# Second mixer's pairs: the inverse's transposed block from a swapped product, four groups per pair, values copied last, ScalarE fading the state

## The reference, cut to what matters

```python
a_mat = where(strict, (k*beta) @ k.T * decay, 0)
t_mat = solve_triangular(a_mat + eye, eye)         # the inverse
u = t_mat @ (v * beta);   w = t_mat @ (k*beta * exp(gc))
def step(state, inp):                              # over the chunks, in order
    v_new = u - w @ state
    o = q_dec @ state + qk @ v_new
    state = state * exp(g_last) + k_dec.T @ v_new  # fade, then add
```

## Time and profile before

| what | value |
|---|---|
| median of 3 runs | 1034.4 us (1032.77 to 1034.87) |
| the profiled execution's own time | 1036.71 us |
| its span in the trace | 1034.9 us |
| mean granted TensorE clock | 0.994 of full |
| busy: PE / DVE / ACT / POOL | 97% / 62% / 42% / 19% |
| pairs of half 0 in the span | about 797.6 to 862 us |
| pairs of half 1 in the span | about 923.0 to 988 us |

### The profile page before, as it was taken

One profiled execution on the slowest core, in us unless ns is written; L12 is line 12 of the kernel. 1 busy time (PEld: TensorE's weight loads), 2 busy tenths in 40 slices (PEclk: granted clock), 3 DMA queues, 4 the chain that ended last, 5 costly groups with the idle time before them and its releaser, 6 DMA issues. The chain is left out here.

```text
span 1034.9 us, 14694 instructions
## 1 busy us (share of the span) xinstructions
PE 1007.5 (97%) x5678; PEld 815.5 (79%) x5678; DVE 645.1 (62%) x1075; ACT 432.9 (42%) x875; POOL 194.1 (19%) x166
## 2 busy tenths in 40 slices
PE   8999999999999999999999999999999998999997
PEld 5888888888776677788878888888888777888886
DVE  4154566622237778767836866686497777967726
ACT  4222323423258863342533343455433466235432
POOL 0011000000001253100100001200203565114692
PEclk9999999999999999999999999999999999989999
DMA  9267634232413252242414346544333212133402
GB/s 320 81 225 259 228 114 151 82 122 82 150 45 113 73 200 101 62 142 82 152 61 160 122 143 231 185 136 144 120 143 123 83 62 85 59 123 105 162 2 81
DMA packets 60820, 132.25 MB, mean 128 GB/s; under 512 B 6096, under 2 KB 6480, under 8 KB 60624
## 3 DMA queue, kind: packets, MB, share of 16 engines
q1 hardware_dynamic: 58304, 118.67, 34.0%
q0 software_dynamic: 2304, 12.58, 3.3%
q10 hardware_dynamic: 144, 0.07, 0.0%
HBM read 117.09 MB, written 14.22 MB: 127 GB/s over the span
## 5 line engine op out<-in xcount | busy, mean ns | idle before, releaser
L289 DVE TENSOR_TENSOR w_lo<-raw,w_hi 128x2048 fp32r<-128x2048 f32 x56 | 132.0, 2357 | 212.1 <-ACT w_hi L285 196.1
L285 ACT ACTIVATE w_hi<-raw 128x2048 fp32r<-128x2048 f32 x51 | 97.4, 1912 | 195.2 <-PE projections_ps L125 156.9
L123 PE MATMUL projections_ps<-projections_x_hi,w_hi 128*128 128x512 f32 x208 | 81.1, 390 | 0.4 <-ACTq L649 0.4
L124 PE MATMUL projections_ps<-projections_x_lo,w_hi 128*128 128x512 f32 x208 | 80.9, 389 | 0.0
L125 PE MATMUL projections_ps<-projections_x_hi,w_lo 128*128 128x512 f32 x208 | 80.9, 389 | 0.0
L123 PE MATMUL projections_ps<-w_hi,projections_x_hi 128*128 128x512 f32 x192 | 74.9, 390 | 0.0
L125 PE MATMUL projections_ps<-w_hi,projections_x_lo 128*128 128x512 f32 x192 | 74.7, 389 | 0.0
L124 PE MATMUL projections_ps<-w_lo,projections_x_hi 128*128 128x512 f32 x192 | 74.7, 389 | 0.0
L246 DVE SCALAR_TENSOR_TENSOR resid<-resid,mixer_cw 128x512 f32<-128x512 f32 x96 | 64.9, 745 | 0.0
L123 PE MATMUL projections_ps<-w_hi,output_m_hi 128*128 128x512 f32 x128 | 51.2, 400 | 2.2 <-DVE resid L1572 1.2
L750 POOL TENSOR_TENSOR tok<-tok,attention_recip 128x512 f32<-128x512 f32 x8 | 8.3, 1043 | 229.8 <-DVE attention_recip L839 229.8
(11 more groups left out here) (371 smaller groups left out, 2416.5 us busy)
## 6 DMA issues: line engine op xcount, KB each, us to landing
raw<-in_w_in SPq DMA_DIRECT2D x26, 1024.0 KB, 5.0
raw<-in_gdn_w_in SPq DMA_DIRECT2D x24, 1024.0 KB, 5.0
tok<-in_ada_w POOLq DMA_DIRECT2D x16, 768.0 KB, 6.4
raw<-in_w_out SPq DMA_DIRECT2D x8, 1024.0 KB, 5.0
qkv_kept<-mixer_ring SPq DMA_DIRECT2D x8, 1024.0 KB, 4.2
mixer_st<-qkv_kept SPq DMA_DIRECT2D x32, 256.0 KB, 2.9
raw<-in_gdn_w_out SPq DMA_DIRECT2D x7, 1024.0 KB, 5.5
resid<-in_att_bias SPq DMA_DIRECT2D x16, 256.0 KB, 2.7
```

The source lines that it names most:

```text
L123: nc.tensor.matmul(out, w_hi, x_hi, start=first, stop=False, skip_group_check=True)
L124: nc.tensor.matmul(out, w_hi, x_lo, start=False, stop=False, skip_group_check=True)
L285: self.nc.scalar.activation(self.hi[s][:], self.raw[s][:], ACT.Copy).then_inc(self.hi_ready, 1)
L289: engine.tensor_tensor(self.lo[s][:], self.raw[s][:], self.hi[s][:], ALU.subtract)\
```

## The change

The transposes "T" and the two scaled copies that follow them are gone. In their place, at level 0, TensorE makes beside each Z0 block a third 32x32 product with its two operands swapped; it gives the off-diagonal block of `T` in the other orientation, and VectorE scales it into `T` with one operation for the whole pair. The diagonal 32x32 blocks of `T` come from `Tc` by two ScalarE activations (`diagonal`), and the block of zeros is set once for each half by GpSimd. Level 1's Z goes to the banks of `psA`, no longer to those of the values. The parts of the next pair move to other slots, and the values are copied at slots 13 and 14. ScalarE multiplies the state by its decay in place (`s_faded`, two activations, chunks 1 and 2), and VectorE only adds, in one operation for both heads.

```diff
-        PARTS = (("V", 0), ("Z", 0), ("T", 0), ("V", 1), ("Z", 1))
-        PRODUCTS_AT = {1: ("Z", 0), 5: ("T", 0), 9: ("V", 1), 13: ("Z", 1)}
-        COPIES_AT = {3: (("Z", 0, 0),), 4: (("Z", 0, 1),), 7: (("T", 0, 0),), 8: (("T", 0, 1),),
-                     14: (("Z", 1, 0), ("Z", 1, 1))}
+        PARTS = (("V", 0), ("Z", 0), ("V", 1), ("Z", 1))
+        PRODUCTS_AT = {1: ("Z", 0), 5: ("V", 1), 9: ("Z", 1)}
+        COPIES_AT = {1: ((0, 0), (0, 1)), 4: ((0, 2),), 9: ((1, 0),), 12: ((1, 1),)}
...
@@ TensorE, double(): waits of V at level 1
-                        pe.wait_ge(t_out, at(i, 2, j, q - 2))
+                        pe.wait_ge(u_ok2, at(i, 4, j, 2))
+                        pe.wait_ge(t_out, at(i, 1, j, 1))
+                        pe.wait_ge(t_diag, at(i, 2, j, 2))
+                        pe.wait_ge(t_zero, i + 1)
...
@@ TensorE, double(): Z at level 0, for each of the 8 blocks
                         for even, odd in BLOCK_PAIRS:
                             mm = nc.tensor.matmul(out[even, odd], V0[odd, m, :], Uc[odd, 8 * j + m, :], ...)
-                    else:
-                        mm = nc.tensor.transpose(out[UP, 0:64], U[j % 2][UP, m, 0:64], ident[UP, 0:64])
+                        even, odd = BLOCK_PAIRS[0]
+                        mm = nc.tensor.matmul(out[odd, 0:32], Uc[odd, 8 * j + m, :], V0[odd, m, :], ...)
...
@@ TensorE, fill(): V0 of pair j + 2
-                            if n == 15 and j + 2 < HB:
+                            if n == 13 and j + 2 < HB:
...
@@ ScalarE
+            def diagonal(i, j):
+                if i or j:
+                    act.wait_ge(v_made, at(i, 4, j - 1, 4))
+                act.wait_ge(tc_ok, 2 * i + (2 if j else 1))
+                for r in range(2):
+                    rows_r = slice(32 * r, 32 * r + 32)
+                    nc.scalar.activation(T[rows_r, :, rows_r], Tc[rows_r, 8 * j:8 * j + 8, :], ACT.Copy).then_inc(t_diag, 1)
...
@@ ScalarE, chunk_part(), behind the two qt activations and ahead of fill(4 * c)
+                    if c < TT - 1:
+                        act.wait_ge(ks_made, at(i, 3, j, c))
+                        act.wait_ge(s_ok, at(i, 3, j, c))
+                        for h in range(2):
+                            nc.scalar.activation(S[:, h, :], S[:, h, :], ACT.Copy,
+                                                 scale=dsel[:, 2, 2 * j + h, c:c + 1]).then_inc(s_faded, 1)
...
@@ ScalarE, fill()
+                            if n == 4:
+                                diagonal(i, j + 1)
-                            if n == 9:
+                            if n == 6:
                                 for grp in range(2):
                                     evacuate(i, j + 1, "V", 1, grp)
-                            if n == 15 and j + 2 < HB:
+                            if n == 13 and j + 2 < HB:
...
@@ GpSimd, once for each half
+                pool.wait_ge(tc_ok, 2 * i + 1)
+                nc.gpsimd.memset(T[0:32, :, 32:64], 0.0).then_inc(t_zero, 1)
...
@@ VectorE, the state in chunks 1 and 2
-                        dve.wait_ge(s_ok, at(i, 5, j, S_COUNT[c]))
-                        for h in range(2):
-                            nc.vector.scalar_tensor_tensor(out=S[:, h, :], in0=S[:, h, :], scalar=dsel[...], in1=psK[:, 2 + h, :], ...)
+                        dve.wait_ge(s_faded, at(i, 4, j, 2 * c))
+                        nc.vector.tensor_tensor(S[:], S[:], psK[:, 2:4, :], ALU.add).then_inc(s_ok, 1)
...
@@ VectorE, fill()
-                            if n in (11, 12):
-                                values_out(i, j + 1, n - 11)
+                            if n in (13, 14):
+                                values_out(i, j + 1, n - 13)
```

More of the change, by code:

```diff
@@ L1817, in second_mixer @@
         v_made, v_out, z_made, u_ok2 = (sem(n) for n in ("v_made", "v_out", "z_made", "u_ok2"))
-        t_made, t_out = sem("t_made"), sem("t_out")
+        t_out, t_diag, t_zero = sem("t_out"), sem("t_diag"), sem("t_zero")
         ks_made, qs_made, ds_made, we_ok = (sem(n) for n in ("ks_made", "qs_made", "ds_made", "we_ok"))
@@ L2179, in double @@
                         if j:
-                            pe.wait_ge(v_out, at(i, 4, j - 1, 2 + grp + 1))
-                    else:
-                        pe.wait_ge(t_out, at(i, 2, j, q - 2))
-                elif kind == "Z":
+                            pe.wait_ge(v_out, at(i, 4, j - 1, 4))
+                        if j > 1:
+                            pe.wait_ge(u_ok2, at(i, 4, j - 1, 4))
+                    else:
+                        pe.wait_ge(u_ok2, at(i, 4, j, 2))
+                        pe.wait_ge(t_out, at(i, 1, j, 1))
+                        pe.wait_ge(t_diag, at(i, 2, j, 2))
+                        pe.wait_ge(t_zero, i + 1)
+                else:
                     pe.wait_ge(v_out, at(i, 4, j, q))
@@ L2211, in double @@
                                                   start=True, stop=True)
-                    else:
-                        mm = nc.tensor.transpose(out[UP, 0:64], U[j % 2][UP, m, 0:64], ident[UP, 0:64])
-                mm.then_inc({"V": v_made, "Z": z_made, "T": t_made}[kind], 1)
+                        even, odd = BLOCK_PAIRS[0]
+                        mm = nc.tensor.matmul(out[odd, 0:32], Uc[odd, 8 * j + m, :], V0[odd, m, :], start=True, stop=True)
+                mm.then_inc({"V": v_made, "Z": z_made}[kind], 1)
             def chunk_products(i, j, c, fill):
@@ L2222, in chunk_products @@
                     for h in range(2):
-                        pe.wait_ge(s_ok, at(i, 5, j, S_COUNT[c] + (h - 1 if c > 1 and j + 1 < HB else 0)))
+                        pe.wait_ge(s_ok, at(i, 3, j, c))
                         mm = nc.tensor.matmul(ks_of(j)[:, h, :], st[:, slot, 1, cols], S[:, h, :], start=True, stop=True)
@@ L2680, in _ @@
                 act.wait_ge(scales_ok, i * 3 + 3)
+                diagonal(i, 0)
                 for grp in range(2):
@@ L3030, in values_out, with doubled @@
                                         rinv[:, j, :].unsqueeze(2).broadcast_to([P, TT, P]), ALU.mult).then_inc(vr_ok, 1)
[L3032 to L3041, removed]
-                                              z_bank(j, grp)[UP].rearrange("p (m c) -> p m c", c=P)[:, :, 64:P]).then_inc(u_ok2, 1)
-                        return
-                    rows_e, cols_o = BLOCK_PAIRS[grp]
-                    nc.vector.tensor_copy(U[j % 2][rows_e, :, cols_o],
-                                          psA.rearrange("p g (m c) -> p (g m) c", c=P)[rows_e, :, cols_o]).then_inc(u_ok2, 1)
+            def doubled(i, j, lv, n):
+                dve.wait_ge(z_made, at(i, 4, j, n + 3 if lv else 2))
+                if lv:
+                    nc.vector.tensor_copy(U[j % 2][UP, 4 * n:4 * n + 4, 64:P],
+                                          z_bank(j, n)[UP].rearrange("p (m c) -> p m c", c=P)[:, :, 64:P]).then_inc(u_ok2, 1)
+                    return
+                both = psA.rearrange("p g (m c) -> p (g m) c", c=P)
+                if n < 2:
+                    rows_e, cols_o = BLOCK_PAIRS[n]
+                    nc.vector.tensor_copy(U[j % 2][rows_e, :, cols_o], both[rows_e, :, cols_o]).then_inc(u_ok2, 1)
+                else:
+                    even, odd = BLOCK_PAIRS[0]
+                    if i or j:
+                        dve.wait_ge(v_made, at(i, 4, j - 1, 4))
+                    nc.vector.tensor_tensor(T[odd, :, even], both[odd, :, even],
+                                            nbp[odd, j].rearrange("p h c -> p (h c)").unsqueeze(2).broadcast_to([32, 8, 32]),
+                                            ALU.mult).then_inc(t_out, 1)
             def chunk_part(i, j, c, fill):
@@ L3072, in chunk_part @@
                     if c:
-                        dve.wait_ge(s_ok, at(i, 5, j, S_COUNT[c]))
-                        for h in range(2):
-                            nc.vector.scalar_tensor_tensor(out=S[:, h, :], in0=S[:, h, :],
-                                                           scalar=dsel[:, 2, 2 * j + h, c:c + 1], in1=psK[:, 2 + h, :],
-                                                           op0=ALU.mult, op1=ALU.add).then_inc(s_ok, 1)
+                        dve.wait_ge(s_faded, at(i, 4, j, 2 * c))
+                        nc.vector.tensor_tensor(S[:], S[:], psK[:, 2:4, :], ALU.add).then_inc(s_ok, 1)
                     else:
@@ L3122, in heads_of @@
                                   21: lambda: w.rest(nc.vector, dve, 1, B_CONV + 3)})
-                for kind in ("Z", "T"):
-                    for grp in range(2):
-                        doubled(i, 0, kind, 0, grp)
+                for n in (2, 0, 1):
+                    doubled(i, 0, 0, n)
                 for grp in range(2):
@@ L3128, in heads_of @@
                 for grp in range(2):
-                    doubled(i, 0, "Z", 1, grp)
+                    doubled(i, 0, 1, grp)
                 for j in range(HB):
```

11 lines of the change are left out of this document (3 added, 8 removed).

## The result

The changed kernel takes 1047.78 us (median of 4 runs, 1046.23 to 1049.06) against 1034.63 (4 runs, 1032.77 to 1037.47): a ratio of 1.0132, 95% interval 1.0115 to 1.0149, 13.2 us slower. Forecast were 1043.8 and a range of 1036.5 to 1050.5. The profiled execution is the fastest of the four: 1046.23, with a span of 1044.2.

A forecast was written before the change was run, and what follows sets the result against it. Each pair was taken as bound by the state's ring (ks, R, W, `we`, ds, S). Half 0's +4.63 and half 1's +4.79 made +9.4 us on the median 1034.4: 1043.8, range 1036.5 to 1050.5.

The forecast's parts named there:

- The wait for the diagonal: Chunk 1 of six pairs: V1 on TensorE waits 1.25 us for ScalarE's diagonal, queued behind qt and the fade.
- The fade: ScalarE's two state activations, queued between qt and the diagonal in chunk 1: 0.53 us of V1's wait.
- Chunk 0: Eight more Z0 products and two VectorE copies ahead of the state's copy make that copy 0.48 us later.
- The values are late: Chunk 3: the next pair's first W waits for VectorE's values, 2.38 us after W instead of 2.95, gaining 0.57.
- Half 0, pair 1: A clip of 1.22 us stands ahead of O; the pair was to cost +0.89 us instead of +1.46.
- rival C: In the pairs: the clock falls behind the new 1.25 us waits; two more falls give 1049.6 us; chance 0.22.
- rival B: Half 1's start: new prologue keeps the clock up, values not late; 1031 with Rival A, kept clock alone 1040.9; chance 0.06.
- Rival A: Chunk 1: the diagonal lands before TensorE wants V1, all six waits go, time 1036.1 us; chance 0.08.
- pair 2 of half 1: GpSimd waits for O, which comes 2.75 us after W instead of 2.86; the pair was to cost +1.92 us.

The follow-up runs named there:

- e1: Changed kernel with ScalarE's diagonal activations one slot earlier (3 instead of 4), ahead of qt and the fade: 1039.46 us, ratio 1.0035.
- e2: Changed kernel with the state faded and added on VectorE in one operation per head, no fade on ScalarE: 1042.74 us, ratio 1.0063.
- e5: Kernel before with only the fade moved to ScalarE and the single addition on VectorE: 1033.22 us, ratio 0.9973.
- e7: e1 with one of the two Z0 copies left ahead of the state's copy, the other moved behind the output's: 1038.94 us, ratio 1.0049.
- e4: e1 with the values copied at VectorE's slots 9 and 13 instead of 13 and 14: 1038.67 us, ratio 1.0041.
- e6: Changed kernel with the first clip of half 0 moved from (1, 10) to (1, 15), the end of its pair: 1044.37 us, ratio 1.0079.
- e8: Changed kernel with diagonal at slot 1, Z0 copies at 1, 3, 4, values at 9 and 13, first clip at (1, 15): 1031.49 us, ratio 0.9976.
- e10: e8 with the first clip back at its old slot (1, 10): 1030.57 us, ratio 0.9966.

## Why the prediction was right, and where it was short

The steps of pair 1 of half 1, by starts of TensorE's products, against the prediction's terms:

| step | before | after | difference | forecast |
|---|---|---|---|---|
| first W to ks | 2.48 | 2.76 | +0.28 | +0.48 |
| ks to W to ds, chunk 1 | 2.45 | 4.41 | +1.96 | +1.74 |
| ds to ks, to chunk 2 | 1.20 | 1.22 | +0.02 | +0.02 |
| ks to W to ds, chunk 2 | 2.90 | 2.93 | +0.03 | 0 |
| ds to ks, to chunk 3 | 1.14 | 1.21 | +0.07 | +0.08 |
| ks to W, chunk 3 | 1.54 | 1.25 | -0.29 | -0.29 |
| W to the next pair's W | 2.95 | 2.44 | -0.51 | -0.57 |
| pair | 14.66 | 16.22 | +1.56 | +1.46 |

- *The wait for the diagonal* was the right mechanism and is the largest term, shown by e1 (taken away, -8.3). Its queue came out to a few hundredths: qt 0.63 after qs begins, the diagonal's end 2.57 after. The size was off by what I left out at the end of it: V1 starts 951.35 - 951.10 = 0.25 after ScalarE is done (e2: 0.25 too). I had set the hand-off to 0.01. Six times, that is 1.5 us. It is not the same for every engine: ks starts 947.98 - 947.92 = 0.06 after VectorE's copy of the state ends.
- *The fade* in that wait, 0.53 forecast, is 0.58 by the starts (950.26 - 949.68), and e2 gives the same. The estimate by the Trainium skill ("ScalarE: Activation LUTs", "What ACT_TABLE_LOAD costs") was 0.59; here the trace agrees. Elsewhere the fade costs 0.04 at most in a pair, and 0.34 in pair 2 of half 0 (e5).
- *Chunk 0* was mis-sized upwards: Z0's result is visible 1.39 after W at the latest, not 1.69: e7's first copy starts there, right behind `w_sb`. The eight products more cost TensorE nothing that can be seen, since ds starts 946.46 - 945.22 = 1.24 after W, and 1.27 before. So only the second copy counts, 0.28, and e7 shows it by moving that copy away.
- *The values are late*: right (next W 2.44 after W of chunk 3, forecast 2.38), and e4 shows it by taking it away.
- *Half 0, pair 1* is the step that failed: "a clip of 1.22 stands ahead of O there". The clip took 2.97, since VectorE had moved against GpSimd's fixed order, from 0.10 ahead of its operation to 2.63 behind. Counted from the pair's first W, the clip came 2.1 later (10.29 before, 12.40 now), by what the pair had lost up to there, and GpSimd's operation 0.6 earlier (10.39 and 9.77). Missing: 1.75, and the fall of the clock behind the idle. GpSimd's timeline of the kernel before had the sign of it, in two operations of one kind, the second beside the clip; no row of the prediction looked at them:

```profile
788.60 4.57 POOL L1859 TENSOR_TENSOR w_lo<-raw,w_hi 128x2048 fp32r<-128x2048 f32 x1 [38.61 <-DVE mixer_Tc L3024]
...
822.69 5.50 POOL L1859 TENSOR_TENSOR w_lo<-raw,w_hi 128x2048 fp32r<-128x2048 f32 x1
```

- *The clock* (rival C, 0.22) came in part: two falls in the pairs, at 828 and 968, for the two of before at 503 and 923. What the one at 968 costs can be read from e6, which has the same order in half 1 and no fall there: its pair 2 lasts 975.89 - 959.49 = 16.40 instead of 17.83.

```profile
975.89 0.61 PE L2239 MATMUL mixer_ps<-mixer_vr,mixer_space 128*128 128x128 f32 x4
```

  So this fall is worth 1.4, not the 2.9 that I took from 923, and it lasted about half as long (968 to 972 against 923 to 929). Without it the pair costs 16.40 - 14.82 = 1.6, where 1.92 was forecast. What decides whether a wait of 1.44 is followed by a fall stays open: of six such waits one was, here and in e6 each, and another one in each. The row at 503, on which C leaned, doesn't decide it either: the same idle of 2.28 stands ahead of the same products in the changed kernel's trace, and no fall follows. Of twelve traces five have a fall there. Only one, the kernel before's, has a fall at 923, and e5 with the same prologue has none. So rival B's reason, that the new prologue keeps the clock up, is not shown: with the old one it can stay up too.
- *Rival A* was false: V1 waited in all six pairs.

The sum of what is shown is 9.4 + 1.5 (hand-offs) - 1.2 (chunk 0) + 0.3 (the smaller steps, six pairs) + 1.75 (clip) - 0.3 (pair 2 of half 1) = 11.4 of the 13.2 between the medians. I put the other 1.8 down to falls: the one at 968 is worth 1.4, the price of the one at 828 isn't measured. The low mean clock of all four runs fits that, but where the falls lie was seen in profiled executions only.

## What to carry to other kernels

When a part is moved to an earlier slot, ask of each of its operands not which engine makes it but what stands ahead of it in that engine's queue at that moment; here the new product was fine, and a copy of 0.84 two places too far back cost 8 us. Add the hand-off between engines to every such chain. Look at the mean clock of each run before you take one execution as the baseline: here it was one of the slower ones, and its falls hid what the forecast lacked. And an order that shifts one engine's work by a few us against another's decides anew which of two large operations that can't run together comes first: look for the operation that is longer than its like.

## What the runs showed of the hardware

- VectorE and GpSimd held each other off when both ran operations with two SBUF inputs. Started second, the clip (128x1024, 1.22 alone) took 2.97, 4.18 and 1.96 and each time ended 1.08 to 1.09 after GpSimd's (changed kernel, e1, e8); started 0.10 and 0.06 first (kernel before, e10), it took 1.22 and GpSimd's 5.50 and 5.55 instead of 4.5. GpSimd's gate (128x1024) took 3.27 instead of 2.36 beside the second clip of pair 2 (kernel before, 843.85). VectorE's 128x256 addition to the state, with one operand in PSUM, kept its 0.42 beside GpSimd's operation (824.02). The Trainium skill ("Advanced Engine Details and Errata", "GPSIMD Details") says that GpSimd shares a read and a write interface with VectorE, in conflict with VectorE's instructions of two SBUF inputs; the traces agree, and in them the one that comes second waits for the whole of the other's operation.
- The state's fade (128x128 from SBUF, scaled by column): two in 0.69, the next activation 0.58 after the first's start.
- From the end of a ScalarE copy to the start of the TensorE product that waited for it passed 0.25 (changed kernel and e2); from the end of VectorE's copy of the state to ks, 0.06.
- A fall of the clock lasted some 4 to 11 us in these traces (968 to 972 here, 825 to 836 in e1). The one from 968 to 972 cost 1.4 us, the one from 923 to 929 cost 2.9.
